# Modulation weights loaded by rows between the projection slabs, the first slab in one float32 pass, the branch gates' weights stationary

## Chip, cores and metric

One of the eight cores of a Trainium2 chip runs the kernel. The metric is the device time of one execution in microseconds (us), taken as the median of some runs of the same program.

## What is computed

Three network blocks in a row on x of 256 tokens by 1024, in float32. The change touches the first block and, at one place, the third.

```python
def first_block(x, c, w_ada, b_ada, ...):
    c_act = jax.nn.silu(c)                                   # 1 x 1024
    mod = c_act @ w_ada + b_ada                              # 1024 x 6144
    shift_m, scale_m, gate_m, shift_f, scale_f, gate_f = jnp.split(mod, 6, axis=-1)
    h = rms_norm(x, g_norm_mix) * (1 + scale_m) + shift_m
    p = h @ w_in                                             # 1024 x 5632: u_f 512, v, b_g, c_g, two gates of 1024
    y_a = fourier_mix(u_f) @ w_fourier                       # DFT over tokens and within groups of 128
    y_b = (b_g * centred_conv3(c_g * v, w_conv)) @ w_conv_out
    z = sigmoid(gate logits a) * y_a + sigmoid(gate logits b) * y_b
    x = x + gate_m * (z @ w_o)
    h2 = rms_norm(x, g_norm_moe) * (1 + scale_f) + shift_f
    x = x + gate_f * expert_choice_moe(h2, ...)              # 16 experts, 32 tokens each, 3 x 8 MB of weights an expert
    return rms_norm(x, g_final)
```

In the third block the NSA mixer projects h to queries, keys, values and 48 branch gates, `gates = sigmoid(proj[..., 2560:2608])`, three for each of 16 heads.

## The kernel before

Each engine has its own instruction stream (the blocks `sync`, `tensor`, `scalar`, `gpsimd`, `vector`), and they meet at semaphores. `make_plan` (L208) writes out by hand the order of TensorE's batches: each entry names a step, a letter for each batch (W takes the next of four work banks in PSUM, A does not), and the batches after which a weight slab's place is free again. `open_bank` waits until the work bank taken four W batches ago has been copied out.

Weights come in slabs of 2.1 MB (two DMAs of 1 MiB each) through a ring of three slots, all issued by SyncE in the order of use. `load` (L725) issues slab n when slab n - 3 has been used: the order of the slabs sets when each load starts, and loads of one queue follow each other. The first norm's x, the constants and other small inputs come over GpSimd's queue.

Products of activations and weights are made of three single-pass float32r matmuls (`mm3`, L915 to L917): the weights' rounded high part comes from ScalarE (`high`, L1745), the low part is the difference, from VectorE (`low`, L2224), each in two halves of 2048 columns. So a slab must have landed, and each half must have passed ScalarE and VectorE, before TensorE uses it. `feature_major3` takes the first half for k < 4 and the second from then on. Plain float32 matmuls go through TensorE as two instructions each.

The modulation, c_act times w_ada, is cut by columns into 12 slabs of 1024 rows by 512 columns (2 KB runs in memory). `modulation(m)` (L1030 on TensorE, the matmul at L1035) multiplies the eight row blocks in four column groups of the array at once, ScalarE copies the 128 x 512 partial sums out, and `modulation_sum(m)` adds them: a product with ones that either spreads a gate over all partitions (L1044) or gives four columns (L1047). VectorE adds the bias (L2284, L2286). In order: slabs 0 and 1 with their sums, norm0 (L937, a transposing product with the row scales), slabs 2 and 3 with their sums, uf (the first 512 columns of w_in, which feed the DFT), the DFT (L1070 to L1077), and in0 to in9 with a modulation slab after every even one and its sum after every odd one. Slab 9 and its sum lie around conv_out, and slabs 10 and 11 between the router's softmax and the expert stage, their sums before and behind the first gather (L1170).

h is made at L1773 by ScalarE twice, as float32 in hT and rounded in h_high; VectorE's h_low (L2302) overwrites hT.

The expert loop streams 384 cells of 1 MiB (8 KB runs) through 16 buffers; `expert_cell` issues them (L771) once what lay in the buffer before is used. The first 16 are issued before the loop. Six of the buffers are the halves of the three ring slots. L1184 are the gate and up products of an expert, L1218 the down products.

In the third block, `nsa_g` (L1526) multiplies each of two token tiles of h, high and low part, as stationary operand with the gate weights as 48 moving columns in plain float32. The rope products for the keys (L1510) follow, then the query projection.

Of the kernel before, what the change touches and what calls it, by code (L numbers as in the profile page):

```python
# [32 lines left out]
P = 128  # L33
# [174 lines left out]
def make_plan():  # L208
    p = Plan()
    for m in range(4):  # L210
        p.add(f"mod{m}a", "W", [0])
        p.add(f"mod{m}b", "W")
        if m == 1:
            p.add("norm0", "AAAA")
    p.add("uf", "WW", [1], split=1)
    p.add("dft_a", "WWWW")
    p.add("dft_b", "WW")
    for s in range(10):
        p.add(f"in{s}", "WW", [1], split=1)
# [14 lines left out]
    p.add("mod10a", "W", [0])  # L234
    p.add("mod11a", "W", [0])
# [3 lines left out]
    p.add("mod10b", "W")  # L239
    p.add("gather0", "WW")  # L240
    p.add("mod11b", "W")
# [31 lines left out]
    for n in range(4):  # L273
# [4 lines left out]
        if n == 0:  # L278
# [4 lines left out]
            p.add("nsa_rope_k", "W" * 3)  # L283
            p.add("nsa_q", "W" * 7, [1, 6], split=2)
# [21 lines left out]
def network(nc, dram, out, const_at, col_at, row_at):  # L306
# [41 lines left out]
    w_nsa_gate = sb("w_nsa_gate", [P, DC, 48])  # L348
# [49 lines left out]
    mod_part_late = A[4][:, 1088:1600]  # L398
# [77 lines left out]
    def split_areas(name, s):  # L476
# [17 lines left out]
        if name in ("uf", "fourier_out", "conv_out", "w_o0", "w_o1") or name.startswith("in"):  # L494
# [13 lines left out]
        if name in ("ple0", "ple1"):  # L508
# [6 lines left out]
                 for h in range(2)]  # L515
    ring_cells = [ring[plan.slab0[name] % NSLOT][:, at:at + 2048]
                  for name in ("w_o1", "mod10a", "mod11a") for at in (0, 2048)]
    cell = [A[2], A[0], A[5], A[1], A[6]] + w_o_areas[0] + w_o_areas[1] + [A[7]] + ring_cells
# [11 lines left out]
    f_up = tmp[1][:, 256:512]  # L530
    r_row = tmp[3][:, 256:512]
# [95 lines left out]
    def wide(a, dim, n):  # L627
# [15 lines left out]
             "out_stored", "low_norm", "x_scaled", "h_even", "relu_done", "h0_copied", "h_scaled", "h2_high", "h2_split", "xT_first", "r_diag", "r_summed", "r_row_ready", "rope_table", "ple_gated")  # L643
# [42 lines left out]
    def _(sp):  # L686
# [57 lines left out]
        def modulation(m):  # L744
            load(f"mod{m}a", 0, two_halves(slot(f"mod{m}a", 0), k_rows(dram("w_ada"), 512 * m, 512), 512))

        for m in range(4):
            modulation(m)
# [7 lines left out]
        modulation(9)  # L756
# [31 lines left out]
        for i in (1, 2):  # L788
            expert_cell(i, 0)
        modulation(10)  # L790
        sp.wait_ge(S["z_ready"], 4)
        for i in (3, 4):
            expert_cell(i, 0)
        modulation(11)
        for i in range(5, NCELL):
            if i in (5, 7):
                sp.wait_ge(products_done, plan.done("w_o0" if i == 5 else "w_o1b", 0))
            if i in (12, 14):
                sp.wait_ge(products_done, plan.done(f"mod{10 + (i - 12) // 2}a", 0))
            expert_cell(i, 0)  # L800
# [84 lines left out]
    def _(pe):  # L885
# [144 lines left out]
        def modulation(m):  # L1030
            w = slab(f"mod{m}a", 0)
            b = open_bank(f"mod{m}a", 0)
            for k in range(DC):
                j = 32 * (k % 4)
                last = mm(b[j:j + 32, :], c_pad[:, k, :], w[:, 512 * k:512 * k + 512], start=(k < 4),  # L1035
                          stop=(k >= 4), tile_position=(0, j), skip_group_check=True)
            batch(last)

        def modulation_sum(m):
            copied(pe, f"mod{m}a", 0)  # L1040
            b = open_bank(f"mod{m}b", 0)
            if m // 2 in (2, 5):
                part = mod_part_late if m == 11 else mod_part
# [2045 lines left out]
```

## Time and profile before

| | us |
|---|---|
| median of 3 runs (lowest to highest) | 2742.43 (2739.89 to 2745.29) |
| the profiled execution | 2740.86 |
| its span in the profile | 2739.1 |
| TensorE busy (PE) | 2424.5 (89%) |
| VectorE busy | 1290.4 (47%) |
| ScalarE busy | 793.3 (29%) |
| DMA bytes | 720.24 MB, mean 263 GB/s |

The profile is of one execution. Its page has 40 slices of 68 us: the granted clock of TensorE in tenths is 8 9 9 9 in the first four and 6 to 8 in the thirteen of the expert stage, and the DMA rate is 328, 207, 262, 311, 409 GB/s in the first five and 421 to 422 in the next twelve. A timeline lists instructions by start, with the time that the engine stood idle before and what released it. The chain of waits is followed back from the last instruction. In a landing row the time runs from a DMA's issue to its completion.

### The profile page before, as it was taken

How to read it: one execution, taken by the hardware profiler on the slowest of the kernel's cores; microseconds unless marked ns; L12 is line 12 of the kernel's file. 1: busy time of each engine (PE TensorE's matmuls, PEld its weight loads, DVE VectorE, ACT ScalarE, POOL GpSimd, SP SyncE). 2: the span in 40 equal slices, each digit the busy share in tenths (PEclk: the TensorE clock that was granted, in tenths of full speed). 3: DMA queues.
4: the chain of work that ended last, by engine and by line, in shares of the span. 5: the costliest groups of instructions: out<-in, count | busy, mean ns of one | idle time of the engine just before them, and what ended most of it. 6: DMA issues, size and time to landing. Idle time of an engine off the chain costs nothing.

```text
span 2739.1 us, 35684 instructions
## 1 busy us (share of the span) xinstructions
PE 2424.5 (89%) x14642; PEld 1708.7 (62%) x14642; DVE 1290.4 (47%) x1861; ACT 793.3 (29%) x1112; POOL 23.0 (1%) x41
## 2 busy tenths in 40 slices
PE   6999877767776767779999999999999999999998
PEld 4998322212121211239899998888968888887887
DVE  2356100000000000025687776877587778777776
ACT  3333000000000000014543334434274334345432
POOL 1000000000000000000000000000000000000000
PEclk8999867687777777789999999999999999999999
DMA  9578999999999999985535554554414555552553
GB/s 328 207 262 311 409 421 422 422 422 422 421 422 422 422 422 422 421 340 201 184 123 184 185 184 169 183 185 169 145 41 154 190 177 201 184 178 76 178 190 116
DMA packets 255640, 720.24 MB, mean 263 GB/s; under 512 B 11256, under 2 KB 129032, under 8 KB 206000
## 3 DMA queue, kind: packets, MB, share of 16 engines
q1 hardware_dynamic: 253616, 708.88, 67.9%
q0 software_dynamic: 1920, 9.88, 0.9%
q8 instruction: 77, 1.26, 0.2%
q14 instruction: 27, 0.22, 0.0%
HBM read 717.65 MB, written 3.16 MB: 263 GB/s over the span
## 4 chain that ended last, share of the span: by engine, by line
PE 53%; issue 41%; DVE 2%; DMA 2%; ACT 1%; POOL 0%; SPq 0%; DVEq 0%; POOLq 0%; ACTq 0%
PE bank L1401 9%; PE bank L915 6%; PE bank L916 6%; PE bank L917 6%; PE bank L1402 5%; PE bank_pair L915 4%; PE bank_pair L916 4%; PE bank_pair L917 4%; PE bank L982 2%; DMA ring<-in_w_in 1%; PE bank L1035 1%; DVE ring_r L2224 1%; PE bank_pair L1572 1%; DMA ring<-in_w_ada 0%; PE bank L1510 0%
## 5 line engine op out<-in xcount | busy, mean ns | idle before, releaser
L1402 PE MATMUL bank<-HT_r,ring_r 128*128 128x256 f32 x1408 | 395.3, 281 | 0.0
L2484 DVE TENSOR_TENSOR A<-bank,A 128x512 f32<-128x512 f32 x16 | 11.1, 692 | 583.6 <-PE bank L1184 583.6
L1402 PEld LDWEIGHTS bank<-HT_r,ring_r 128*128 128x128 f32 x1408 | 266.4, 189 | 0.7
L917 PE MATMUL bank<-HT_r,ring_r 128*128 128x256 f32 x904 | 255.7, 283 | 0.0
L1401 PE MATMUL bank<-HT_r,AB_r 128*128 128x512 f32 x640 | 228.9, 401 | 2.2 <-DVE HT_r L2232 2.2
L1401 PE MATMUL bank<-HT_r,AC_r 128*128 128x512 f32 x640 | 226.3, 398 | 0.0
L1184 PE MATMUL bank<-ring,A 128*32 128x512 f32 x768 | 147.4, 858 | 85.2 <-DMA ring<-in_w_gate_e 48.6
L2224 DVE TENSOR_TENSOR ring_r<-ring,AB_r 128x2048 fp32r<-128x2048 f32 (+1 forms) x81 | 179.8, 2260 | 76.8 <-ACT AB_r L1745 76.8
L2224 DVE TENSOR_TENSOR ring_r<-ring,A_r 128x2048 fp32r<-128x2048 f32 (+1 forms) x93 | 201.0, 2194 | 27.7 <-ACT A_r L1745 27.7
L2224 DVE TENSOR_TENSOR ring_r<-ring,AC_r 128x2048 fp32r<-128x2048 f32 x66 | 148.5, 2289 | 75.5 <-ACT AC_r L1745 75.3
L917 PE MATMUL bank_pair<-A_r 128*128 128x512 f32 x472 | 183.7, 389 | 0.0
L916 PE MATMUL bank_pair<-ring_r,A_r 128*128 128x512 f32 x448 | 174.5, 389 | 0.0
L1964 ACT ACTIVATE tmp<-tmp 128x256 f32<-128x256 f32 x112 | 46.9, 418 | 437.1 <-DVE tmp L2768 321.0
L917 PEld LDWEIGHTS bank<-HT_r,ring_r 128*128 128x128 f32 x904 | 173.5, 192 | 0.0
L1745 ACT ACTIVATE AB_r<-ring 128x2048 fp32r<-128x2048 f32 (+1 forms) x81 | 148.6, 1883 | 83.6 <-DMA ring<-in_w_in 33.8
L1745 ACT ACTIVATE A_r<-ring 128x2048 fp32r<-128x2048 f32 (+1 forms) x93 | 166.6, 1830 | 15.1 <-DMA ring<-in_w_out 11.9
L1704 ACT ACTIVATE A<-bank 128x256 f32<-128x256 f32 (+1 forms) x69 | 30.2, 448 | 450.0 <-PE bank L1191 302.3
L2265 DVE TENSOR_REDUCE tmp<-bank 128x256 f32<-128x512 f32 x176 | 120.9, 687 | 65.4 <-PE bank L1402 65.3
L1833 ACT ACTIVATE A<-bank 128x512 f32<-128x512 f32 x16 | 9.6, 597 | 484.8 <-PE bank L1184 484.8
L915 PE MATMUL bank_pair<-A_r 128*128 128x512 f32 x384 | 149.7, 390 | 0.0
L1745 ACT ACTIVATE AC_r<-ring 128x2048 fp32r<-128x2048 f32 x66 | 123.2, 1916 | 88.7 <-DMA ring<-in_ffn_w_gu 77.9
L1184 PEld LDWEIGHTS bank<-ring,A 128*32 128x32 f32 x768 | 17.9, 125 | 208.4 <-DMA ring<-in_w_gate_e 107.7
(529 smaller groups left out, 4793.8 us busy)
## 6 DMA issues: line engine op xcount, KB each, us to landing
ring<-in_ffn_w_gu SPq DMA_DIRECT2D x88, 1024.0 KB, 6.8
ring<-in_w_up_e SPq DMA_DIRECT2D x48, 1024.0 KB, 26.6
ring<-in_w_gate_e SPq DMA_DIRECT2D x48, 1024.0 KB, 26.7
ring<-in_w_down_e SPq DMA_DIRECT2D x48, 1024.0 KB, 26.8
ring<-in_w_in SPq DMA_DIRECT2D x46, 1024.0 KB, 7.4
ring<-in_ffn_w_down SPq DMA_DIRECT2D x40, 1024.0 KB, 6.1
A<-in_w_gate_e SPq DMA_DIRECT2D x32, 1024.0 KB, 26.6
A<-in_w_up_e SPq DMA_DIRECT2D x32, 1024.0 KB, 26.9
```

The costliest lines, as they stand in the source:

```text
L915: mm(out_, lhs[0], rhs[0], start=start, stop=False, skip_group_check=True)
L916: mm(out_, lhs[0], rhs[1], start=False, stop=False, skip_group_check=True)
L917: return mm(out_, lhs[1], rhs[0], start=False, stop=stop, skip_group_check=True)
L982: last = mm(b[:, f * T:(f + 1) * T], w[:, at:at + P], src[:, k, :], start=(k == 0), stop=(k == n_k - 1))
L1184: last = mm(b[32 * j:32 * j + 32, :], xe_now[:, k, :], w[:, 512 * j:512 * j + 512], start=(k == 0), stop=(k == DC - 1), tile_position=(0, ...
L1401: mm(both, high, h_both[:, :, k, :], start=(k == 0), stop=False, skip_group_check=True)
L1402: last = mm(both[:, 1, :], low, h_high[:, k, :], start=False, stop=(k == DC - 1), skip_group_check=True)
L1704: frees(run(dst, work_bank(name, i)[0:rows_, 0:n], ACT.Copy, scale=scale), name, i)
L1745: run(area[:, :], w[:, at:at + area.shape[1]], ACT.Copy).then_inc(S["high_ready"], 1)
L1964: run(f_act[b % 2], f_conv[b % 2], fn).then_inc(S["gelu_done"], 1)
L2224: v.tensor_tensor(twins[f"ring{slot}"][:, part], ring[slot][:, part], area[:, :].bitcast(fp32), ALU.subtract).then_inc(S["low_ready"], 1)
L2265: frees(v.tensor_reduce(dst, both, AX.X, ALU.add), name, i)
```

## The change

- The modulation is cut by rows instead: slab s of group g has rows 256 s to 256 s + 255 and columns 2048 g to 2048 g + 2047, as two DMAs of 128 rows with runs of 8 KB. Four column groups of the array hold four blocks of 512 columns, and one PSUM bank a group collects all eight row blocks: a work bank for group 0, banks 0 and 1 for groups 1 and 2. One copy out and one sum a group: four products with four columns picked from the identity, and for groups 1 and 2 two products of 32 rows that spread a gate.
- Group 0 comes first, with norm0 behind its third slab. Groups 1 and 2 come one slab after each of in0 to in7, with their sums after in4's and in8's place. Nothing of the modulation is left behind in9.
- uf is one plain float32 pass, with hT, and w_in's first slab is not split. h_high is made behind hT by four wider copies, and h_low behind uf's last batch.
- The first 16 expert cells lie in other buffers and are issued at other points.
- The branch gates: the gate weights are split once and are the stationary operand, with 48 columns; h streams as 256 columns in three passes, the 48 x 256 result is copied out and turned back by two transposes.

```diff
 def make_plan():
     p = Plan()
-    for m in range(4):
-        p.add(f"mod{m}a", "W", [0])
-        p.add(f"mod{m}b", "W")
-        if m == 1:
+    for s in range(4):
+        p.add(f"mod0_{s}", "A" if s else "W", [0])
+        if s == 2:
             p.add("norm0", "AAAA")
-    p.add("uf", "WW", [1], split=1)
+    p.add("mod0", "W")
+    p.add("uf", "WW", [1])
     p.add("dft_a", "WWWW")
     p.add("dft_b", "WW")
     for s in range(10):
         p.add(f"in{s}", "WW", [1], split=1)
-        p.add(*((f"mod{4 + s // 2}a", "W", [0]) if s % 2 == 0 else (f"mod{4 + s // 2}b", "W")))
+        if s < 8:
+            p.add(f"mod{1 + s // 4}_{s % 4}", "A", [0])
+        if s in (4, 8):
+            p.add(f"mod{s // 4}", "WWW")
     p.add("fourier_out", "WWWW", [3], split=1)
-    p.add("mod9a", "W", [0])
     p.add("conv_out", "WWWW", [1, 3], split=2)
-    p.add("mod9b", "W")
...
+        def modulation(g, s):                       # SyncE
+            name, w = f"mod{g}_{s}", dram("w_ada")
+            dst = ring[slot(name, 0)][:, :].rearrange("p (k n) -> p k n", k=2)
+            load(name, 0, [(dst[:, a, :], w[(2 * s + a) * P:(2 * s + a + 1) * P, 2048 * g:2048 * g + 2048])
+                           for a in range(2)])
...
         for s in range(10):
             dense(f"in{s}", w_in, 1, 512 + 512 * s)
-            if s % 2 == 0:
-                modulation(4 + s // 2)
+            if s < 8:
+                modulation(1 + s // 4, s % 4)
...
+        for i in range(1, NCELL):
+            if i == 3:
+                sp.wait_ge(products_done, plan.done("conv_out", 3))
+            if i == 5:
+                sp.wait_ge(S["z_ready"], 4)
+            if i in (7, 11):
+                sp.wait_ge(products_done, plan.done("w_o0" if i == 7 else "w_o1b", 0))
             expert_cell(i, 0)
...
+        def modulation(g, s):                       # TensorE
+            w = slab(f"mod{g}_{s}", 0)
+            for a in range(2):
+                k = 2 * s + a
+                for j in range(4):
+                    at = 2048 * a + 512 * j
+                    last = mm(mod_bank[g][32 * j:32 * j + 32, :], c_pad[:, k, :], w[:, at:at + 512], start=(k == 0),
+                              stop=(k == DC - 1), tile_position=(0, 32 * j), skip_group_check=True)
+            batch(last)
+
+        def modulation_sum(g):
...
+            b = open_bank(f"mod{g}", 0)
+            for c in range(4):
+                last = mm(b[:, 4 * c:4 * c + 4], mod_part[:, c * P:(c + 1) * P], pick_rows, start=True, stop=True)
             batch(last)
+            for h in range(2 if g else 0):
+                j = 32 * (h if g == 1 else 2 + h)
+                b = open_bank(f"mod{g}", 1 + h)
+                batch(mm(b[:, :], ones[j:j + 32, :], mod_part[j:j + 32, :], start=True, stop=True,
+                         tile_position=(j, 0), skip_group_check=True))
...
-                    pe.wait_ge(S["h0_split"], k // 2 + 1)
-                last = mm3(b[:, :], h_parts(k, t * P, P), w(512 * k, 512), k == 0, k == DC - 1)
+                    pe.wait_ge(S["h0_copied"], k // 2 + 1)
+                last = mm(b[:, :], hT[:, k, t * P:(t + 1) * P], w[:, 512 * k:512 * k + 512], start=(k == 0),
+                          stop=(k == DC - 1))
...
-        modulation(10)
-        modulation(11)
...
-        modulation_sum(10)
...
-        modulation_sum(11)
...
         b = open_bank("nsa_g", 0)
-        for t in range(TT):
-            for k in range(DC):
-                for part in range(2):
-                    last = mm(b[:, t * 48:(t + 1) * 48], h_parts(k, t * P, P)[part].bitcast(fp32),
-                              w_nsa_gate[:, k, :], start=(k + part == 0), stop=(k + part == DC))
+        for k in range(DC):
+            last = mm3(b[0:48, 0:T], (g_w_high[:, k, :], g_w_low[:, k, :]), h_parts(k), k == 0, k == DC - 1)
         batch(last)
...
+        copied(pe, "nsa_g", 0)
+        b = open_bank("nsa_gT", 0)
+        for t in range(TT):
+            last = nc.tensor.transpose(b[:, t * 48:(t + 1) * 48], g_rows[:, t * P:(t + 1) * P], ident[0:48, 0:48])
+        batch(last)
...
-        modulated_gain(g_mix, range(4), 8, "g_norm_mix")
-        low("uf", 0)
+        modulation(0, 0, 4)
+        modulated_gain(g_mix, (0,), 8, "g_norm_mix")
+        low("in0", 0)
+        filled(dve, "uf", 1)
...
+            if s == 4:
+                modulation(1, 2, 2)
...
         low("fourier_out", 0)
         dve.wait_ge(S["conv_ready"], 1)
-        modulation(8)
+        modulation(2, 0, 2)
+        modulated_gain(g_moe, (1, 2), 32, "g_norm_moe")
```

## Rows read from the trace of the kernel before

**Rows 1.** Busy time by stretch (us, each engine's busy us, granted clock, DMA share, GB/s)

```profile
32.00:34.00 2.00, 1.38 (x16) 0.17 (x8) 0.00 (x0) 0.55 (x1) 0.00 (x0) 1.00 1.06 390
...
100.00:120.00 20.00, 20.00 (x163) 17.95 (x162) 9.83 (x7) 10.20 (x9) 0.00 (x0) 1.00 0.60 213
...
285.00:290.00 5.00, 5.00 (x29) 1.18 (x32) 3.73 (x16) 1.49 (x2) 0.00 (x0) 0.62 0.73 262
290.00:400.00 110.00, 86.61 (x540) 26.07 (x532) 9.75 (x35) 5.27 (x10) 0.00 (x0) 0.77 1.01 421
```

**Rows 2.** Timeline of the start (start us, us, engine, line, operation, idle before and releaser)

```profile
22.46 5.44 PE L937 MATMUL bank_pair<-diag,x 128*128 128x128 f32 x32 [0.23 <-DVE diag L2215]
...
27.83 1.92 PE L1035 MATMUL bank<-ring,tmp 128*32 128x512 f32 x16
...
34.10 1.05 PE L1047 MATMUL bank<-ones,tmp 128*128 128x1 f32 x8 [0.72 <-ACT tmp L1704]
...
34.91 3.71 ACT L1745 ACTIVATE AB_r<-ring 128x2048 fp32r<-128x2048 f32 x2 [0.86 <-DMA ring<-in_w_in]
...
42.09 0.77 PE L915 MATMUL bank<-AB_r,HT_r 128*128 128x512 f32 x1 [6.95 <-DVE HT_r L2302]
...
55.37 0.60 ACT L1704 ACTIVATE A<-bank 128x512 f32<-128x512 f32 x1 [4.84 <-PE bank L917]
```

**Rows 3.** The chain that ended last, projections and router (start us, us, what)

```profile
56.06 7.12 PE bank L1070 x16
...
92.82 0.86 PE bank L1044 x2
...
105.45 1.85 PE bank L1035 x16
...
144.93 0.79 PE bank L1047 x8
...
209.68 1.85 PE bank L1035 x16
...
274.08 0.96 PE bank L1150 x2
```

**Rows 4.** Weight loads: landings of slabs in4, in2, in8 and w_o0, in this order

```profile
DMA to landing us min/median/max: 5.1/6.3/7.4
...
DMA to landing us min/median/max: 5.0/6.9/8.8
...
DMA to landing us min/median/max: 6.0/7.5/9.0
...
DMA to landing us min/median/max: 8.6/9.8/10.9
```

**Rows 5.** VectorE's timeline: second splits of in8, then both of conv_out

```profile
171.04 2.28 DVE L2224 TENSOR_TENSOR ring_r<-ring,A_r 128x2048 fp32r<-128x2048 f32 x1
...
207.44 4.48 DVE L2224 TENSOR_TENSOR ring_r<-ring,AB_r 128x2048 fp32r<-128x2048 f32 x2
```

**Rows 6.** Busy time by stretch again: the clock after gaps, and at the ropes

```profile
43.00:44.00 1.00, 1.00 (x4) 0.73 (x3) 0.00 (x0) 1.00 (x4) 0.00 (x0) 0.50 1.18 487
...
264.00:265.00 1.00, 0.41 (x4) 0.44 (x5) 0.44 (x1) 0.52 (x1) 0.00 (x0) 1.00 0.53 115
...
1904.00:1905.00 1.00, 1.00 (x7) 1.00 (x6) 0.84 (x2) 0.97 (x4) 0.00 (x0) 0.50 1.07 412
...
1949.00:1951.00 2.00, 2.00 (x5) 1.13 (x5) 0.00 (x0) 1.44 (x3) 0.00 (x0) 0.50 0.94 262
```

**Rows 7.** Timeline of all engines at the first expert

```profile
283.38 2.05 PE L1044 MATMUL bank<-A,ones 128*128 128x512 f32 x2
...
285.37 1.94 PE L1184 MATMUL bank<-AC,A 128*32 128x512 f32 x8
```

**Rows 8.** The chain that ended last, at the branch gates and ropes

```profile
1941.64 7.89 PE bank L1526 x64
...
1949.53 5.19 PE bank L1510 x6
```

More of the change, by code:

```diff
@@ L493, in split_areas @@
             return [(0, t_["AB"][:, 0:2048])]
[L494 removed]
+        if name in ("fourier_out", "conv_out", "w_o0", "w_o1") or name.startswith("in"):
             if (plan.split0[name] + s) % 2 == 0:
@@ L742, in loop @@
                     load(name, s, slab(s, it), after=plan.slab_end[n - NSLOT] + (it - 1) * len(plan.kinds[name]))
[L744 to L748, printed above, removed]
+        def modulation(g, s):
[3 more added lines that the diff above has]
+                           for a in range(2)])
+        for s in range(4):
+            modulation(0, s)
         w_in = dram("w_in")
@@ L1029, in _ @@
         pe.wait_ge(S["c_pad_ready"], 1)
-        def modulation(m):
-            w = slab(f"mod{m}a", 0)
-            b = open_bank(f"mod{m}a", 0)
-            for k in range(DC):
-                j = 32 * (k % 4)
-                last = mm(b[j:j + 32, :], c_pad[:, k, :], w[:, 512 * k:512 * k + 512], start=(k < 4),
-                          stop=(k >= 4), tile_position=(0, j), skip_group_check=True)
-            batch(last)
[L1039 to L1043, printed above, removed]
-                last = mm(b[:, :], ones[:, :], part[:, :], start=True, stop=True)
-            else:
-                for c in range(4):
-                    last = mm(b[:, c:c + 1], mod_part[:, c * P:(c + 1) * P], ones[:, 0:1],
-                              start=True, stop=True)
+        mod_bank = [open_bank("mod0_0", 0), bank[0], bank[1]]
@@ L1049, in modulation_sum @@
             batch(last)
-        for m in range(4):
-            modulation(m)
-            modulation_sum(m)
-            if m == 1:
+            for h in range(2 if g else 0):
[3 more added lines that the diff above has]
+                         tile_position=(j, 0), skip_group_check=True))
+        for s in range(4):
+            modulation(0, s)
+            if s == 2:
@@ L1055, in _ @@
                 first_normT()
-        w = split_slab("uf", 0)
+        pe.wait_ge(ident_loaded, 16)
+        modulation_sum(0)
+        w = slab("uf", 0)
         for t in range(TT):
@@ L1756, in _, with modulation @@
         run(c_act, col("c", 0, 8), ACT.Silu).then_inc(S["c_act_ready"], 1)
-        def modulation(m):
-            copy_out(f"mod{m}a", 0, (mod_part_late if m == 11 else mod_part)[:, :])
-        modulation(0)
         act.wait_ge(x_loaded, 16)
         squares(0)
-        for m in range(1, 4):
-            modulation(m)
-        high("uf", 0)
+        filled(act, "mod0_3", 0)
+        frees(run(mod_part[:, :], work_bank("mod0_0", 0)[:, :], ACT.Copy), "mod0_0", 0)
+        def modulation(g):
+            filled(act, f"mod{g}_3", 0)
+            run(mod_part[:, :], bank[g - 1][:, :], ACT.Copy).then_inc(S["mod_copied"], 1)
         act.wait_ge(S["mod_ready"], 1)
@@ L1771, in _ @@
                 k = 2 * g + c
-                for dst in (hT[:, k, :], h_high[:, k, :]):
-                    ins = run(dst, bank[g][:, c * T:(c + 1) * T], ACT.Identity,
-                              scale=g_mix[:, k:k + 1], bias=modc[:, k:k + 1])
+                ins = run(hT[:, k, :], bank[g][:, c * T:(c + 1) * T], ACT.Identity,
+                          scale=g_mix[:, k:k + 1], bias=modc[:, k:k + 1])
             ins.then_inc(S["h0_copied"], 1)
+        for g in range(4):
+            act.wait_ge(S["h0_copied"], g + 1)
+            run(h_high[:, 2 * g:2 * g + 2, :], hT[:, 2 * g:2 * g + 2, :], ACT.Copy).then_inc(S["h0_high"], 1)
         high("in0", 0)
@@ L2351, in _ @@
         dve.wait_ge(S["conv_ready"], 1)
-        modulation(8)
+        modulation(2, 0, 2)
+        modulated_gain(g_moe, (1, 2), 32, "g_norm_moe")
+        for g in (1, 2):
+            for h in range(2):
+                copied(dve, f"mod{g}", 1 + h)
         for s in range(6, 10):
@@ L2381, in _ @@
                 low("w_o0", 0)
-        modulation(9)
-        modulated_gain(g_moe, range(4, 10), 32, "g_norm_moe")
         low("w_o1", 0)
@@ L2500, in _ @@
         select(0)
-        modulation(10)
         stage("gather0", 0, 0)
-        modulation(11)
-        for m in (10, 11):
-            copied(dve, f"mod{m}b", 0)
         for half in range(2):
```

109 lines of the change are left out of this document (52 added, 57 removed).

## The prediction

> **What bounds the kernel now.** I read the busy time by stretch first. In the projections TensorE is busy 20.00 of 20 us, while the DMA engines have a share of 0.60. In the expert loop the DMA engines are full (1.01, 421 GB/s) and TensorE is not (86.61 of 110 us) [rows 1]. So there are three regimes. From 0 to about 42 us the first loads and the modulation decide. From there to the first expert TensorE's own queue decides. Then come 384 expert cells at the DMA rate, and after them TensorE again. The expert loop's length is 368 MiB at 421 GB/s, some 917 us, and the change doesn't touch its bytes, so an earlier first expert moves its end one for one. The loop has 16 cells loaded ahead. In 285 to 290 us the DMA rate drops to 262 GB/s [rows 1]: the cells were full, and the DMA waits for the first expert. So the work ahead of the experts counts in full, if the 16 cells are there in time. The second and third blocks behind the loop are bound by TensorE, where the branch gates' matmuls lie in the chain [rows 8].
>
> **The start (to the DFT).** Before: the last modulation sum ends at 34.10 + 1.05 = 35.15 us, the first projection's weights have landed at 34.91, ScalarE and VectorE split them, and the first product starts at 42.09 [rows 2]; it ends when ScalarE's copy starts, 55.37 [rows 2], less 0.04. After: no split of these weights, half as many ScalarE copies of h, and plain float32. What is late next is TensorE's own order: the third slab, norm0, the fourth slab, one sum. The DMA moved 390 GB/s here with 2 KB rows, against 421 in the expert loop with 8 KB rows [rows 1], so a slab of 2.1 MB takes 5.0 instead of 5.4 us. The weights landed at 34.91 as the fifth slab; the third is two slabs earlier less what shares the queue, about 22 us in the new kernel (an estimate from these rates). Behind it: slab 1.9, norm0 5.4, slab 1.9 [rows 2], copy 0.6, sum 1.05, the two small VectorE steps 0.6, the first two ScalarE copies of h, 256 columns each, 0.9 (one of 512 takes 0.60 [rows 2]), so 22 + 12.4 = 34.4 us. The weights are there by 34.91 - 4 x 0.4 = 33.3, so they don't bind. The product itself is 16 float32 matmuls as 32 instructions at 7.12 / 16 = 0.445 us [rows 3], 14.2 us, against 13.2 for the 48 single ones (part of them at half clock). It ends at 48.6 against 55.33: **-6.7 us**. Bounds: the start 33.3 to 36.1 (the third slab at half clock, twice 1.9 us), and half clock for the first 4 us, as the product of before had it after a gap of 7 us [rows 6], costs 2.1. The new gap is 1.4 us. So -7.8 to -2.9.
>
> In the Trainium skill, "DMA: Bandwidth & Descriptors", Specifications, line rate is reached from 512 B a transfer up. By that rule 8 KB rows would give nothing over 2 KB; the rates above differ by 8%. By the rule the weights would land at 34.9 and the start would be 0.5 us later.
>
> **Work in the projections.** A modulation slab costs TensorE 1.85 us, a sum 0.86 (a gate, spread over partitions) or 0.79 [rows 3]. Before, between the DFT and fourier_out: 5 slabs, 2 and 3 sums, 13.3 us, and a stall of 0.2. After: 8 slabs (8 matmuls each in four column groups, as before, so 1.85), and 2 sums of 0.79 + 2 x 0.86 = 2.5: 19.8 us. **+6.3 us**, since TensorE is full here.
>
> **The wait that is added.** A load is issued when the slab three places earlier is done. Before, from in2 on, a projection slab never stood behind a modulation slab. Its second half landed 7.4 us after its own issue, 7.8 after the first half's; a half takes ScalarE 1.9 and VectorE 2.25 us to split [rows 2, 4, 5]. After, from in2 to in8, the modulation slab is issued when in_s is done, and in_(s+2) only 1.85 us later, behind it on the same queue. The trace of before has this once: w_o's slab is issued 1.88 us after conv_out's (released by 209.68 + 1.85 [rows 3]), and its second half lands 10.9 us after its issue instead of 7.4 [rows 4]. With the 8 KB rows of the slab ahead (0.4 us less) I take 10.9 from the first issue. Then the first half is split 10.9 + 0.1 + 1.95 + 2.3 = 15.3 us after the issue, the second at 17.5. TensorE has a slab of 11.7 (93.68 to 105.45 [rows 3]) and 1.85 to do: it wants the first half at 13.6 and the second 12 products (1.46 us) later. The stall is 1.7 + 0.8 = 2.5 us. It gives the next slab 2.5 us of slack, so it comes in every second one: in2, in4, (a sum of 2.5 shields in5 and in6), in7: 7.5 us. Before, in8's landing of 9.0 us [rows 4] shows the chain at its edge: VectorE's split ended at 173.33 [rows 5] and TensorE stalled 0.2. in2's was 8.8. If these are the slabs' own times, both stand behind a modulation slab in the new kernel and 1.4 + 1.5 us are added, if not, little. I take half, 1.4. Two smaller waits: the third sum of the first group needs the bank that VectorE frees only after it has split in5, 0.6 us; and in9's second half needs the bank of the second group's sum, which VectorE copies only behind the conv casts and fourier_out's split, 1.3 us. Together **+10.8 us**; bounds 0 (were the loads shared or faster) and +17 (with the clock, below).
>
> The same page of the Trainium skill, Anatomy of one DMA, fits a DMA as 2.0 us and its bytes at 436 GB/s. By that four MiB in a row land after 11.6 us, an estimate, thus 9.8 from the later issue, and the three stalls would be 1.1 us shorter each.
>
> **To the experts.** The slab and sum between fourier_out and w_o go, 1.85 + 0.79. But conv_out's split ends on VectorE 13.9 us after fourier_out's start (207.44 + 4.48 [rows 5]), and TensorE, without the cover, wants it at 13.1: **-1.0 and -0.8 us**. In the router's tail the two slabs lay beside VectorE's top-k; only the mask transpose comes earlier, by the 0.96 us of the bias row's product, which the slabs had pushed in front of it at 274.08 [rows 3]. The sum before the gather lay beside VectorE. The one after it, 2.05 us at 283.38, held the expert (285.37) by 1.1 us past its ready operand [rows 7]; but without slabs and sums TensorE has less to do there and its clock may be lower in the gather. Sum of the tail: **-1.0 us** (bounds -2.1 and 0). The 16 cells are issued earlier (nine waited for w_o's last product, five will; four fewer are 10 us at 421 GB/s) and don't bind.
>
> **The branch gates.** Before: 32 float32 matmuls with 48 columns, 7.89 us, and behind them three rope products take 5.19 us for 6 instructions, 0.87 each [rows 8], at a granted clock of 0.50 [rows 6]; the same form takes 0.445 at full clock [rows 3]. After: 24 single-pass matmuls of 256 columns, 0.12 us each (11.7 / 96), 2.9 us; TensorE stays dense and I expect full clock, 2.7 us for the ropes; two transposes 0.3. 13.1 becomes 5.9: **-7.1 us**. The added ScalarE and VectorE split of 384 columns (some 0.5 us each) falls beside TensorE's key and value slabs, where both have gaps; if it held TensorE it would cost 1 us. VectorE's later steps there start on the ropes and move along. Bounds: -4.5 (half clock stays) to -7.5.
>
> **Sum.** -6.7 + 6.3 + 10.8 - 1.0 - 0.8 - 1.0 - 7.1 = +0.5 us. The profiled execution took 2740.9 us (span 2739.1), so 2741.4; it stood 1.5 us under the median of 2742.4, so I forecast **2742.9 us**, no change that can be measured.
>
> **Rivals.** (1) The loads cover themselves: the modulation slab's 8 KB rows are out of the way sooner, or the two share the engines, and nothing stalls. For it: the DMA share was only 0.60. Against it: w_o's landing. The sum is -10.3, 2732.1 us, faster. (2) The stalls cost clock too. After a gap of 1.9 us, from 1901.1 to 1903.0, TensorE was granted 0.50 for some 3.2 us; after one of 1.7 us, to 264.6, it was not [rows 6]. My stalls are 1.7 us long, at that edge. Four of them at 1.6 us, and 2.1 us in the float32 product, give +8.5: 2751.4 us, slower. It decides from gaps of about 1.9 us on. (3) The rope products stay at half clock: +2.6, 2745.5, still no change. That the gate edit doesn't do what it says has little room: the forms are those of the projections.
>
> **How the numbers follow.** A measurement here can tell some 0.2%, 5.5 us. My forecast, with what differs by less than that (rival 3 too): 0.47, its own range 2737 to 2748. Rival 1, whole or in large part: 0.29. Rival 2, or stalls longer than reckoned: 0.24. So faster 0.29, same 0.47, slower 0.24. The range reaches to both rivals: 2732 to 2751.
>
> **What would show it.** In the new profile: the first float32 product starting at 34 to 35 us and the DFT at 49 to 50; waits of TensorE on VectorE's split of in2, in4 and in7 of some 2.5 us each, with landings near 10.5 us; fourier_out starting near 208 instead of 198; the first expert near 293; the gate products 3 us and the ropes behind them at clock 1.00. If the landings stay at 7.5, rival 1 holds; if the granted clock is 0.50 after the stalls, rival 2. A first expert before 285 us would make the sum wrong.

## The result and the profile after

The changed kernel takes 2747.1 us (median of 19 runs, 2743.2 to 2752.9) against 2742.1 us (19 runs, 2739.8 to 2745.6) for the kernel before: a ratio of 1.0019, 95% interval 1.0013 to 1.0026. That is 5.1 us more, just under the 0.2% that was called no change. Beside the later experiments it was run again: 2745.3 against 2740.9, ratio 1.0017, interval 1.0007 to 1.0026.

The profiled execution took 2748.7 us (span 2747.0), 7.9 us over the profiled one of before. So the table below holds some 3 us that the medians don't have.

| stage, us | before | after | difference |
|---|---|---|---|
| start, to in0's first product | 67.4 | 62.3 | -5.1 |
| in0 to fourier_out's first product | 130.5 | 150.1 | +19.6 |
| fourier_out to the first expert | 87.5 | 89.5 | +2.1 |
| gates' products and three ropes | 13.1 | 5.7 | -7.4 |
| all else | | | -1.3 |

TensorE's timeline in the profile after: the first slab, the DFT, the first product after each of the two longest waits for in2 and in4, the first expert, and the ropes with the transposes behind them (start us, us, engine, line, operation, idle before and its releaser).

```profile
34.62 15.67 PE L1071 MATMUL bank<-ring,HT 128*128 128x512 f32 x32 [1.61 <-ACT HT L1789]
51.02 5.39 PE L1080 MATMUL bank<-consts,A 128*128 128x512 f32 x12 [0.73 <-issue]
...
92.45 0.39 PE L915 MATMUL bank<-HT_r,AB_r 128*128 128x256 f32 x1 [2.83 <-DVE ring_r L2243]
...
123.50 0.39 PE L915 MATMUL bank<-HT_r,AB_r 128*128 128x256 f32 x1 [1.93 <-DVE ring_r L2243]
...
301.99 1.94 PE L1198 MATMUL bank<-AC,A 128*32 128x512 f32 x8 [0.99 <-DVE A L2497]
...
1958.76 2.74 PE L1523 MATMUL bank<-AC,consts 128*128 128x512 f32 x6
1961.43 0.32 PE L1547 MATMUL bank<-consts,tmp 48*128 48x48 f32 x2
```

The first product starts at 34.62 where the kernel before had 42.09 [rows 2]; the DFT at 51.02 where it had 56.06 [rows 3]; the first expert at 301.99 instead of 285.37 [rows 7]; the ropes take 2.7 us instead of 5.2 [rows 8].

Busy time by stretch in the projections (us, busy us of PE, PEld, DVE, ACT, POOL with counts, granted clock, DMA share, GB/s), the kernel after:

```profile
60.00:80.00 20.00, 20.00 (x158) 18.12 (x157) 5.88 (x4) 5.99 (x6) 0.00 (x0) 1.00 0.24 86
80.00:90.00 10.00, 9.62 (x81) 7.98 (x80) 0.00 (x0) 1.84 (x2) 0.00 (x0) 1.00 0.78 277
90.00:100.00 10.00, 7.12 (x46) 6.85 (x47) 4.49 (x2) 2.84 (x4) 0.00 (x0) 0.83 1.00 392
120.00:130.00 10.00, 7.88 (x55) 6.28 (x48) 4.50 (x2) 4.38 (x5) 0.00 (x0) 0.83 0.93 352
150.00:160.00 10.00, 8.59 (x71) 6.75 (x70) 5.70 (x4) 3.71 (x2) 0.00 (x0) 1.00 0.62 233
170.00:180.00 10.00, 8.52 (x68) 8.31 (x69) 8.58 (x11) 3.25 (x6) 0.00 (x0) 1.00 0.99 393
```

Before, TensorE was full here at clock 1.00 [rows 1]. Now it idles by 1.4 to 2.9 us in four of these stretches, and in two of them the clock is 0.83: a third of the stretch was spent at 1.2 GHz instead of 2.4. The waits of TensorE between 60 and 300 us, after (engine and line, what was waited for, us in total, times, longest):

```profile
PE bank L915 <- DVE ring_r L2243: 10.5, 11, 2.8
PE bank L1169 <- DVE tmp L2458: 2.9, 1, 2.9
PE bank L1141 <- DVE x L2416: 1.7, 1, 1.7
```

and the loads from 60 to 200 us, after (what, count, KB each, median us from issue to landing):

```profile
ring<-in_w_in SPq DMA_DIRECT2D x16, 1024.0 KB, 9.5
ring<-in_w_ada SPq DMA_DIRECT2D x14, 1024.0 KB, 6.5
```

The same view and stretch of the kernel before:

```profile
ring<-in_w_in SPq DMA_DIRECT2D x16, 1024.0 KB, 6.7
ring<-in_w_ada SPq DMA_DIRECT2D x10, 1024.0 KB, 10.6
```

The one that is issued behind the other lands late, and the change swapped them. in2's halves after, issued from 76.1 on behind a modulation slab of 74.3, landed in this time:

```profile
DMA to landing us min/median/max: 8.3/9.9/11.5
```

In the kernel before in2's were 5.0 to 8.8 [rows 4].

### The profile page after: what moved, and what is told of

The parts are those of the page before. It is cut to its first block, busy times and chain, and to the rows that moved or that the text cites. A ratio compares the mean times of both kernels' runs of the same rounds, so it can differ in the third digit from the quotient of the medians.

```text
span 2747.0 us, 35477 instructions
## 1 busy us (share of the span) xinstructions
PE 2428.9 (88%) x14548; PEld 1701.1 (62%) x14548; DVE 1285.2 (47%) x1855; ACT 783.3 (29%) x1099; POOL 23.0 (1%) x41
## 4 chain that ended last, share of the span: by engine, by line
PE 54%; DMA 23%; SPq 10%; issue 8%; DVE 3%; ACT 1%; DVEq 0%; POOLq 0%; POOL 0%; ACTq 0%
SPq L776 10%; PE bank L1414 9%; DMA AB<-in_w_gate_e 6%; PE bank L915 6%; PE bank L916 6%; PE bank L917 6%; PE bank L1415 5%; PE bank_pair L915 4%; PE bank_pair L916 4%; PE bank_pair L917 4%; DMA ring<-in_w_gate_e 4%; DMA AB<-in_w_up_e 3%; PE bank L982 2%; DMA A<-in_w_gate_e 2%; DMA ring<-in_w_down_e 2%
## 5 line engine op out<-in xcount | busy, mean ns | idle before, releaser
L1198 PE MATMUL bank<-ring,A 128*32 128x512 f32 x768 | 140.2, 818 | 71.9 <-DMA ring<-in_w_up_e 40.0
L1761 ACT ACTIVATE A_r<-ring 128x2048 fp32r<-128x2048 f32 (+1 forms) x92 | 164.6, 1829 | 14.7 <-DMA ring<-in_w_out 11.5
L1720 ACT ACTIVATE A<-bank 128x256 f32<-128x256 f32 (+2 forms) x68 | 29.8, 446 | 447.4 <-PE bank L1205 304.6
L915 PE MATMUL bank<-HT_r,AB_r 128*128 128x256 f32 x472 | 137.1, 291 | 9.7 <-DVE ring_r L2243 8.4
```

Source lines behind the costliest of these rows:

```text
L915: mm(out_, lhs[0], rhs[0], start=start, stop=False, skip_group_check=True)
L1198: last = mm(b[32 * j:32 * j + 32, :], xe_now[:, k, :], w[:, 512 * j:512 * j + 512], start=(k == 0), stop=(k == DC - 1), tile_position=(0, ...
L1761: run(area[:, :], w[:, at:at + area.shape[1]], ACT.Copy).then_inc(S["high_ready"], 1)
```

## The experiments

Every kernel was also profiled once. "Over before" and "under before" are against the runs of the kernel before on the same chip in the same hour, 2740.6 to 2742.5 us in median.

### The gates alone

```diff
+        for k in range(DC):
+            last = mm3(b[0:48, 0:T], (g_w_high[:, k, :], g_w_low[:, k, :]), h_parts(k), k == 0, k == DC - 1)
```

> The kernel before with the branch-gate edit alone. Theory (the gates part gives about 7.5 us, nearly half of it because the ropes behind it run at the full clock, and nothing later takes it back): 2734.6, 7.5 under before; the third block's key and value part ends at the same time as before, the six ropes behind it at clock 1.00 in 2.6 us. Rival A (only the products get cheaper, the ropes stay at 1.2 GHz): 4.6 under, 2737.5. Rival B (the time is given back at the queries): no difference.

Measured: 2731.9 against 2742.3 us, ratio 0.9961, interval 0.9947 to 0.9974, thus 10.5 under before (7 to 14.5). TensorE's timeline behind the key and value products, with this edit:

```profile
1942.45 0.28 PE L921 MATMUL bank<-HT_r,w_nsa_gate_r 128*48 128x256 f32 x1
1942.57 2.73 PE L1514 MATMUL bank<-AC,consts 128*128 128x512 f32 x6
1945.23 0.32 PE L1538 MATMUL bank<-consts,tmp 48*128 48x48 f32 x2
1945.49 0.39 PE L919 MATMUL bank<-HT_r,A_r 128*128 128x256 f32 x1
```

The gates' first product stands at 1939.81, the queries at 1945.49: 5.7 us instead of 13.1. So the gates give 7.4 us, 2.7 of it through the ropes' clock; rival A (4.6) and B (none) fall. The rest of this profile's 10.2 us lies elsewhere, 1.7 ahead of the gates and 1.1 behind, where the two kernels are the same; the interval takes in 7.4. All profiles together say how much of it is chance. From the first expert to the end took 2453.4 to 2453.7 us in the three without the gates' edit (before, and the next two runs), and 2441.7 to 2447.5 in the eleven with it, mean 2445.1: 8.5 less. The profile of the gates alone is the lowest of the eleven.

### The rows without the gates

The changed kernel with the old code in the branch gates, all else kept.

> The changed kernel without the branch-gate edit, so the modulation by rows and the plain first slab alone. Theory (the edits add up, and what the changed kernel gained at the gates it had lost before the first expert): 12.6 over before, 2754.7. Rival (most of what the tail before the first expert lost, about 4 us, was a chance drop of the clock in the one profiled run): about 8 over in the median, 2750, and the first expert's shift spread over the runs.

Measured: 2754.6 against 2742.3 us, ratio 1.0045, interval 1.0029 to 1.0061: 12.3 over before, near the theory's 12.6. The interval goes from 8 to 17, so it doesn't exclude the rival's 8. The gates' products and the first ropes, in this kernel:

```profile
1954.60 8.29 PE L1535 MATMUL bank<-w_nsa_gate,HT_r 128*128 128x48 f32 x64
1962.70 2.04 PE L1519 MATMUL bank<-AC,consts 128*128 128x512 f32 x2
```

With the gates' 7.4 us from the traces the two edits add up: 12.3 less 7.4 is 4.9, and 5.1 was measured. With the 10.5 between medians they give 1.8; the intervals are too wide to tell these apart. And the rival was right about the profile: here the way from fourier_out to the first expert took 86.7 us, not the 89.5 of the changed kernel's own profile, with the same code.

### The plain first slab alone

The rounding of h and its low part stand behind the copies of h here too, as in the changed kernel; the product itself:

```diff
-                last = mm3(b[:, :], h_parts(k, t * P, P), w(512 * k, 512), k == 0, k == DC - 1)
+                last = mm(b[:, :], hT[:, k, t * P:(t + 1) * P], w[:, 512 * k:512 * k + 512], start=(k == 0),
+                          stop=(k == DC - 1))
```

> The kernel before with the first slab in plain float32 alone (modulation in its old order, by columns). Theory (ACT starts its eight copies at 34.9 as before, one instruction a chunk instead of two; the uf products start near 36 instead of 42.1 and take about 15.7 us, most of them at 1.2 GHz): in0 starts near 63.8 instead of 67.8, 4 us under before, 2738.1. Rival A (at the full clock): 6 under, 2736. Rival B (in0's weights or h_low come last, since their work is moved behind uf): no gain, 2742.

Measured: 2740.2 against 2742.3 us, ratio 0.9989, interval 0.9981 to 0.9998: 2.1 under before, half of the expected 4. Its first product:

```profile
36.70 16.97 PE L1062 MATMUL bank<-ring,HT 128*128 128x512 f32 x32 [1.71 <-ACT HT L1778]
```

It starts 5.4 us earlier than before, as expected, but lasts 17.0 us: at the full clock 32 instructions are 14.2 us (0.445 each, from [rows 3]), so 2.8 us are half clock. in0 starts at 65.7, 1.7 us earlier than before and not the expected 4, so 3.4 of the changed kernel's 5.1 us come from the modulation by rows. That share moves with the clock: in the two profiles further down with this slab and the gates' edit, in0 starts at 65.1 and 64.9, which leaves 2.6 to 2.8 us for the rows. The first loads also moved faster by rows, 423 GB/s from 8 to 20 us in the changed kernel against 390 in the kernel before; how much of the gain is that was not tried.

### Thin modulation loads

```diff
-            load(name, 0, [(dst[:, a, :], w[(2 * s + a) * P:(2 * s + a + 1) * P, 2048 * g:2048 * g + 2048])
+            n = 128 if g else 2048
+            load(name, 0, [(dst[:, a, 0:n], w[(2 * s + a) * P:(2 * s + a + 1) * P, 2048 * g:2048 * g + n])
```

> The changed kernel with the eight modulation slabs of the projections loading 128 of each row's 2048 columns; their products read x in place of the slab, so the second and third pass of the modulation are left out and TensorE has the same instructions. Theory (the loads of in2 to in8 land late because a modulation slab is ahead of them in the queues): the waits for the split slabs, 10.5 us, and the half clock behind two of them, 2 to 3 us, go; fourier_out starts near 199.5 instead of 212.7 and the median is 12 to 13 under the changed kernel, about 2734.5. Rival (TensorE itself is longer there, through the banks and the extra products): fourier_out stays within 3 us of 212.7, the median at 2744 to 2747.

Measured: 2735.1 against 2742.3 us, ratio 0.9971, interval 0.9961 to 0.9981; that is 12 us under the changed kernel, as expected. The products of these slabs read x in place of the slab, so this kernel leaves out the second and third pass of the modulation. Its waits from 60 to 300 us:

```profile
PE bank L1171 <- DVE tmp L2460: 2.9, 1, 2.9
PE bank L916 <- DVE small L2304: 2.4, 1, 2.4
...
PE bank L916 <- DVE ring_r L2245: 0.6, 2, 0.5
```

Its projection loads from 60 to 200 us:

```profile
ring<-in_w_in SPq DMA_DIRECT2D x16, 1024.0 KB, 6.6
```

The projection weights land after 6.6 us again, and the waits for split slabs shrink from 10.5 to 0.6 us with TensorE's instructions unchanged: the stalls came from the bytes queued ahead. The place of the gain was missed in part. fourier_out starts at 205.3, not near 199.5: once in9 is reached early, its second half waits 2.4 us for the bank that VectorE has yet to empty of the second group's sum (the 1.3 us of the prediction; hidden in the changed kernel's first profile, 1.1 us in its second), and the clock falls for 3.4 us behind that wait, and for 3.4 us at 134 us, behind the first group's sum, where TensorE had waited for nothing (some 1.7 us each time). The rest of the 12 us lies in the way from fourier_out to the experts, 85.4 us here and 89.5 in the changed kernel's profile; the next runs are about that. They show that this rest is not the loads': beside the changed kernel's second profile, below, the thin loads save 8.0 us up to fourier_out and nothing on that way, so 2 to 4 of the 10 to 12 us between the medians (2735.1 against 2745.3 and 2747.1) have no place that a trace shows.

### The changed kernel again, and with filler

> The changed kernel once more, beside the next three. Theory (its tail from the end of fourier_out to the first expert varies by some us with where the clock falls, 73.7 to 77.9 us in the profiled runs so far, whatever the modulation): a median of 2745 to 2748 and a tail under 77.8. Rival (the row order costs the tail 2 us or more each time): a tail of 77.8 again.

Measured: 2745.3 us, as above. Its first expert:

```profile
298.62 1.94 PE L1198 MATMUL bank<-AC,A 128*32 128x512 f32 x8 [0.99 <-DVE A L2497]
```

From fourier_out's first product it is 85.4 us to there, against 89.5 in the first profile of the same kernel (the expectation counts from fourier_out's end, some 11.7 us later, and holds: under 77.8). All of the difference lies ahead of the transposes of the router's probabilities, where the first profile had 10.6 us at clock 0.50 and this one 0.3. So the loss of 2 us in the table's third row isn't the change's.

```diff
+        for t in range(TT):
+            for h in range(2):
+                for _ in range(4):
+                    mm(acc[t][h][:, :], zeros[:, 0:P], zeros[:, :], start=False, stop=False, skip_group_check=True)
         b = open_bank("bias_row", 0)
```

> The changed kernel with sixteen products of zeros added to the residual banks where the two modulation slabs stood in the kernel before, so that TensorE is busy there. Theory (the two slabs had kept the clock up, and without them the gather and the tail run at 1.2 GHz): the clock is at 1.00 in parts of the 20 us ahead of the first expert, which comes 2 to 4 us earlier, and the median is 2 to 4 under the changed kernel. Rival (the clock falls there anyway, as it did in the kernel before from 280 on): within 1 us of the changed kernel.

Measured: 2745.5 us (ratio 1.0013, interval 1.0004 to 1.0022), level with the 2745.3 beside it. Busy time from the transposes of the router's probabilities to the first expert, the changed kernel again:

```profile
282.09:298.62 16.53, 11.28 (x44) 8.74 (x45) 6.46 (x23) 0.59 (x1) 0.58 (x1) 0.50 0.51 213
```

and the same stage with filler, whose products of zeros take 4.0 us from 289.2 on:

```profile
288.83:304.57 15.74, 13.35 (x60) 9.69 (x61) 6.46 (x23) 0.59 (x1) 0.58 (x1) 0.72 0.53 219
```

The clock did rise, and the stage is 0.8 us shorter, not 2 to 4: the filler lies in a time in which TensorE waited 2.9 us for VectorE, and the way to the mask's transposes, 5.25 us, stayed as long as it was. The whole way from fourier_out is 86.4 us against 85.4, since the clock fell ahead of the filler (at 276 us) where in the other profile it didn't. The median shows no gain, so the rival is nearer the truth: without the two slabs this stage does run at 0.50 throughout, but that costs little.

### Spaced modulation slabs

```diff
         for s in range(10):
             feature_major3(f"in{s}", 0, 0, h_parts if s else h0_fresh, src=h_parts)
-            if s < 8:
-                modulation(1 + s // 4, s % 4)
-            if s in (4, 8):
-                modulation_sum(s // 4)
+            if s % 2 == 0:
+                modulation((2 + s) // 8 + 1, (1 + s // 2) % 4)
+            if s == 5:
+                modulation_sum(1)
```

Besides, one slab ahead of the DFT, one behind fourier_out, one behind conv_out, and the last sums in the middle of w_o's first half.

> The changed kernel with the eight later modulation slabs spaced so that at most every second projection slab has one behind it: one ahead of the DFT, one after in0, in2, in4, in6 and in8, one after fourier_out and one after conv_out; the last sums stand in the middle of the w_o product. Theory (the stalls come from a modulation load ahead of every projection load, not from the form of the rows): no wait for split slabs over 0.5 us, fourier_out starts near 193, 5 us earlier than in the kernel before, and the median is 2729 to 2733, 14 to 18 under the changed kernel. Rival (loads by whole rows are slow or disturb whatever their order): at least two waits of 1.5 us or more stay, 2738 or more.

Measured: 2746.3 against 2740.9 us, ratio 1.0022, interval 1.0013 to 1.0031: a miss by some 15 us. The stalls did go: waits for split slabs fell to 0.5 us, and in0 to fourier_out took 131.4 us instead of 150.1. What took their place, first on TensorE at the DFT:

```profile
60.24 9.06 PE L1089 MATMUL bank<-consts,A 128*128 128x512 f32 x16 [9.36 <-ACT A L1733]
```

then on ScalarE ahead of it:

```profile
55.46 3.71 ACT L1774 ACTIVATE AB_r<-ring 128x2048 fp32r<-128x2048 f32 x2 [15.74 <-DMA ring<-in_w_in]
59.08 1.06 ACT L1733 ACTIVATE A<-bank 128x512 f32<-128x512 f32 x2
```

and the landing of in0's weights, issued at 31.7:

```profile
DMA to landing us min/median/max: 20.1/21.7/23.3
```

The DMA engines are full in the first 55 us. From 31 to 55 us they moved 386 GB/s, so one more slab there, 2.1 MB, is 5.4 us of them, and it put in0's slab a step behind: it landed near 55 us, and ScalarE, which makes in0's high part first, sat 15.7 us ahead of the two copies of uf that the DFT needs. The wait had moved from in2 to the DFT, through an engine that was nowhere near busy. The way from fourier_out to the first expert also grew, to 95.2 us, with two slabs and the sums there now.

> The kernel with spaced modulation slabs, and ACT copies the uf and DFT results before it makes in0's high part instead of after. Theory (what that kernel lost was 9.4 us at the start, where ACT waited for in0's weights, late behind the one modulation slab moved ahead of the DFT, with the copies that the DFT needs queued behind): the DFT starts near 52, in0 near 64.5 instead of 73.5, the median is 8 to 9 lower, 2737 to 2738. Rival (in0 itself is bound by its weights, which landed 10 us late): in0 starts at 66 or later, the median at 2740 or more.

This is the same kernel with ScalarE's order turned. VectorE's order was turned with it: in0's low part is now made behind the low part of h, not ahead of it. ScalarE's part of the edit:

```diff
-        high("in0", 0)
         for t in range(TT):
             copy_out("uf", t, uf[:, t, :])
         for g in range(4):
             copy_out("dft_a", g, dft_v[:, g, :])
+        high("in0", 0)
```

Measured: 2737.4 against 2740.6 us, ratio 0.9987, interval 0.9978 to 0.9996; 9 us under the kernel without it, and 8 under the changed kernel. ScalarE copies uf at 50.27 instead of 59.08, and TensorE's DFT starts at 52.02:

```profile
50.27 0.60 ACT L1733 ACTIVATE A<-bank 128x512 f32<-128x512 f32 x1 [6.27 <-PE bank L1079]
52.02 7.13 PE L1089 MATMUL bank<-consts,A 128*128 128x512 f32 x16
```

in0 starts at 64.0. VectorE too starts h's low part at 50.27, which had stood behind in0's before. So the loss of the kernel without this edit was what stood in the engines' queues behind in0's split, not the late weights as such; for the DFT it was ScalarE's queue, since the DFT needs its copies alone. What VectorE's turn adds for in0 wasn't run by itself. The 2729 to 2733 expected of the spaced kernel are missed even so: fourier_out starts at 197.8, and from there it is 93.5 us to the first expert.

### The good parts together

> The kernel before with the two edits that are free of the modulation's order, the branch gates and the plain first slab. Theory (they add up: 7.5 and 2): 2732.5, 9.5 under before. Rival (the gates alone gave 10.5, and both give 12.5): 2729.5.

Measured: 2729.4 against 2740.9 us, ratio 0.9957, interval 0.9943 to 0.9970, thus 11.5 under before; the interval (8 to 16) holds both the theory's 9.5 and the rival's 12.5. Then the first modulation pass by rows was added to it (four slabs of 256 rows and one sum, as in the changed kernel; the other eight slabs stay by columns, where the kernel before has them):

> The kernel before with the branch gates' edit, the plain first slab, and the modulation by rows for its first pass alone; the eight later modulation slabs stay by columns where the kernel before has them. Theory (by rows is a gain of 2.7 us at the start, in0 from 65.1 to 62.4, and all that it loses it loses among the projections): 2726.7, 2.7 under the kernel with the two edits alone (2729.4), fourier_out 5 us earlier than in the kernel before, at 192. Rival (the earlier start is given back by in0's or in1's weights, which are loaded behind): no difference to 2729.4.

Measured: 2732.2 against 2740.6 us, ratio 0.9960, interval 0.9946 to 0.9974: 8.5 under before and not the expected 14. In the profile, in0 started at 62.3 and fourier_out at 192.7, 2.3 us earlier than without the rows, as expected; the first expert came 1.2 us later (92.2 us from fourier_out against 88.7). Both were run again, side by side:

> The kernel before with the branch gates' edit and the plain first slab, again, beside the next one. Both theories: 2729 to 2732.

> The same with the first modulation pass by rows, again, on the same chip as the run ahead of it. Theory (in the profiled run of this kernel fourier_out started 2.3 us earlier than in the one without rows, and only the clock in the tail before the experts, 92.8 us against 89.3, took it back by chance): 1 to 3 us under the other, and a tail under 91 in the profile. Rival (an earlier start costs the tail its clock each time): level with the other, the tail at 92 or more again.

Measured: 2732.0 and 2729.4 against 2742.5 us, ratios 0.9964 (0.9951 to 0.9978) and 0.9955 (0.9942 to 0.9969), and 88.7 and 89.2 us from fourier_out to the first expert. The last two profiles also show what the clock is worth ahead of the experts. From the transposes of the router's probabilities to the first expert, the kernel with the rows' first pass, first and second profile:

```profile
268.17:284.87 16.70, 16.25 (x81) 8.80 (x81) 6.96 (x23) 1.78 (x3) 0.58 (x1) 0.70 1.01 421
```

```profile
267.48:281.53 14.05, 13.55 (x80) 6.45 (x81) 6.96 (x24) 1.78 (x3) 0.58 (x1) 0.86 1.01 425
```

The same code with the two slabs in it took 2.7 us less when the clock was 0.86. With the slabs TensorE is full here (16.25 of 16.70 us), so the clock counts in full; without them it isn't (11.28 of 16.53).

The second pair speaks for the rows' first pass by 2.6 us, the first against it by 2.7; the ten runs of each, taken together, have the same median, 2730.2 us. Its 2.3 us are seen in both traces up to fourier_out, and not in the total. Either kernel beats the kernel before, by 8 to 13 us in these four medians, and the changed one by 15 to 17 (2730.2 against 2745.3 and 2747.1).

## Why the prediction came out as it did

The forecast of 2742.9 us, no change that can be measured, was 4.2 us under the measured 2747.1, and the range of 2732 to 2751 held it. Step by step, with the size each was given and what the runs show. The profiles of the changed kernel, its second one, and the one without the gates' edit have the same code up to the experts, so each stage can be read three times (for the way to the experts the thin loads' profile is a fourth). The kernel with filler has the same code up to the router, and its profile, 6 us slower than the next of its eleven runs, stands apart.

| step | forecast | shown |
|---|---|---|
| start | -6.7 | -5.1 (-5.1, -5.0, -5.2; with filler -3.3) |
| projections | +6.3 + 10.8 = +17.1 | +19.8 (19.6, 20.3, 19.4; with filler 23.5) |
| fourier_out to the experts | -1.0 - 0.8 - 1.0 = -2.8 | -2.5 |
| branch gates | -7.1 | -7.4 |
| sum | +0.5 | +4.8 |

- **The start: right in its mechanism, 1.7 us too much.** The first product was forecast at 34.4 and came at 34.62. The term that was off is its length, 14.2 us at the full clock, where 15.67 were measured, with the clock at 0.50 from 35.9 to 39.3 us. The prediction had this half clock as a bound of 2.1 us and put it at nothing in its sum. In the spaced kernel the same 32 instructions took 13.97 us, in the one with filler 16.69, in the one with the plain slab alone 16.97.
- **The stalls: right in total, wrong in their places, so the total is in part luck.** Forecast were 2.5 us each at in2, in4 and in7 and 1.4 for in2 and in8. Shown are 3.3 at in2, 1.9 at in4, 1.4 at in6, 1.7 at in7 and 1.6 at in8, 10 us in all. Of the two smaller waits, the 0.6 us at the first group's sum shows in no profile of the changed kernel, and the 1.3 at in9 in the second alone (1.1). in2's second half landed 11.5 us after its issue, against the 10.9 taken from w_o's slab [rows 4]: that was the right row to price it by. In the Trainium skill, "DMA: Bandwidth & Descriptors", Anatomy of one DMA, the fit gave 9.8 from that issue, an estimate; the trace disagrees: in2's took 1.7 us more than that and in3's 0.7 (10.5). The page gives the fit for single DMAs issued through GpSimd, and these are SyncE's, queued one behind the other.
- **The clock behind the stalls: the step that failed.** The forecast counted it as nothing and left it to rival 2. In the profile after it fell to 0.50 for 3 to 4 us behind the waits of 2.83 and 1.93 us, and the two stretches at 0.83 cost 1.7 us each (a third of 10 us at half speed), 3.4 us; with 6.3 of added work and 9.9 of waits that is 19.6, what that profile shows. Rival 2 had the mechanism and, for these waits, the length from which it acts (1.9 us), but counted on four stalls long enough for it; in the three profiles there were two, two and three. In the filler's there were four such stretches, one of them behind no wait, and +23.5 us. What actually happened lies between forecast and rival. With the start's 1.7 us, this one omission, TensorE at 1.2 GHz behind gaps of 1.6 to 2.8 us, is 5.1 us, more than the 4.3 between the two sums; waits 0.9 us shorter than forecast took part of it back.
- **Rival 1 is refuted.** The landings did not stay at 7.5 us, and with thin loads, where they do, the time is 12 us lower. The number it gave, 2732.1, is close to that kernel's 2735.1.
- **The way to the experts: right, though the one profile said otherwise.** The profiled pair shows +2.1 us. Over all profiles with the old order of this stage (seven, with the gates', the start's or the first pass's edits elsewhere) it took 87.5 to 92.2 us, mean 89.3; over the four with the new, 85.4 to 89.5, mean 86.8. The two ranges overlap; where the clock stood at 1.00 for all but 0.3 us up to the transposes of the router's probabilities it is 87.5 (the kernel before) against 85.4 (two profiles), 2.0 less. The profile of before was the shortest of its kind and that of after the longest. Without the repeats, the 5 us between forecast and profile would have been put down to the two removed slabs and their clock; the filler, which gave much of the clock back and 0.8 us, shows that this would have been a wrong story.
- **The gates: right.** 5.7 us instead of the forecast 5.9, the ropes at clock 1.00 as forecast; rival 3 is refuted. The casts on ScalarE and VectorE were hidden, as was said.

Of the signs named, the gates' came as said; fourier_out came at 212.5 us and not near 208, the first expert at 302.0 (298.6 in the second profile) and not near 293. The near match of the last row (4.8, and 5.1 between the medians) says less than it seems: single stages moved by 4 us between profiles of the same code.

What stays open: of the 10.5 us of the gates alone 7.4 are explained. Over all profiles the part behind the first expert is 8.5 shorter with the edit, so about 1 us has no known place, and the other 2 are most likely the chance of that run, whose interval begins at 7. Nor is it shown why the plain first slab runs at half clock for 0 to 3 us behind gaps that are all near 1.6 us.

## What to carry over

Interleaving extra slabs into a stream of weight loads costs twice: TensorE's own instructions, and the place in the DMA queue, since a load issued right behind another of 2.1 MB landed 3 us later (9.5 against 6.7 in median) though the DMA engines were idle a third of the time; with one such slab at every second projection slab no wait for them was over 0.5 us. Move an operand load only after reading which engine's in-order queue will stand behind it: one slab moved into the full first 55 us held the DFT for 9.4 us through two small ScalarE copies. And read a stage in several profiles of the same code before explaining a few us of it; here the same 87 us varied by 4.

## What the runs showed of the hardware

The granted clock behind waits was regular in part. In five profiles of the projections (the changed kernel twice, without the gates' edit, with thin loads, with filler) TensorE's waits of 1.93, 1.99, 2.04, 2.08, 2.31, 2.43, 2.76, 2.83, 2.99, 3.09 and 3.12 us were each followed by 3 to 4 us at 0.50, and none of those of 0.5 to 1.75 us was. It isn't a matter of the wait's length alone. The gap of 1.61 us ahead of the first slab was followed by 0.50 in eight profiles and not in the spaced kernel's. And the clock fell behind the first group's sum: with thin loads (134.0 to 137.4 us) and with filler (143.1 to 146.5) without any wait, in the two spaced kernels behind waits of 1.23 and 1.37 us inside that sum, and in the other three profiles with a sum there not at all.

From the transposes of the router's probabilities to the first expert the clock was 0.50 all the way in six profiles without the two slabs, and for 9.8 or 9.9 us of 16.7 in six of seven with them. What it is worth there depends on how full TensorE is: 0.8 us with products of zeros in place of the slabs, since TensorE waits for VectorE's small steps (2.9 us for one of them, in the waits above), and 2.7 us with the slabs, where it doesn't.
